# Where the weight slots start in SBUF: byte 64 modulo 128 in every stage instead of in the narrow stages alone

## The reference, cut to what matters

```python
def layer(x, ctx, c, c_ctx, ...):                    # first block, twice
    sh1, sc1, gt1, sh2, sc2, gt2 = adaln(c, w_ada, b_ada)   # silu(c) @ w_ada, 1024 x 6144
    px = modulate(rms_norm(x, g1), sh1, sc1) @ w_in         # 1024 x 1536, for ctx too
    ...                                              # attention, Fourier mix, spatial gate
    x = x + gt1 * (mix @ w_out)                      # 1024 x 1024
    h = modulate(rms_norm(x, g2), sh2, sc2)
    x = x + gt2 * (square(relu(h @ w1)) @ w2)        # 1024 x 4096, 4096 x 1024

def second_block(x, ...):                            # twice
    proj = rms_norm_2(x, attn_norm_g) @ w_in         # 1024 x 3656
    ...                                              # three kinds of causal attention
    x = x + mix @ w_out                              # 1024 x 1024
    h2 = rms_norm_2(x, ffn_norm_g)
    x = x + (silu(h2 @ w_gate) * (h2 @ w_up)) @ w_down   # 1024 x 2816 (two), 2816 x 1024
```

## Time and profile before

| | |
|---|---|
| median of three executions | 1592.0 us |
| the profiled execution | 1594.35 us, span 1592.6 us, mean granted TensorE clock 0.991 |
| TensorE matmuls busy | 1541.2 us, 97% of the span |
| TensorE weight loads busy | 1262.6 us (beside the matmuls) |
| VectorE, ScalarE, GpSimd busy | 1028.4, 795.5, 114.2 us |
| DMA | 322.41 MB, mean 202 GB/s |

### The profile page before, as it was taken

The page is one execution under the profiler, slowest core; times in us unless marked ns, Lnnn a source line. Parts: engine busy times, 40 slices in busy tenths (PEclk is TensorE's granted clock), DMA queues, the critical chain, the costliest instruction groups (busy, mean ns, idle before and its releaser), DMA issues.

```text
span 1592.6 us, 23486 instructions
## 1 busy us (share of the span) xinstructions
PE 1541.2 (97%) x9164; PEld 1262.6 (79%) x9164; DVE 1028.4 (65%) x1577; ACT 795.5 (50%) x1356; POOL 114.2 (7%) x130
## 2 busy tenths in 40 slices
PE   6999999999999999998999999999999999999999
PEld 2864689778888887567898878779998787689987
DVE  3637756455456437576785576978995558879973
ACT  3537735343345225565664456645554456555542
POOL 0111000010001000100000031010000111000000
PEclk9999999999999999999999999999999999999999
DMA  9528623487568524586998689436665596356653
GB/s 360 152 84 313 215 75 114 145 264 253 162 220 277 162 66 133 176 279 190 335 319 300 211 272 312 160 108 183 191 197 191 184 326 227 106 141 192 198 190 115
DMA packets 201005, 322.41 MB, mean 202 GB/s; under 512 B 14576, under 2 KB 100864, under 8 KB 200768
## 3 DMA queue, kind: packets, MB, share of 16 engines
q1 hardware_dynamic: 192992, 293.51, 57.6%
q0 software_dynamic: 7680, 27.34, 4.8%
q10 hardware_dynamic: 224, 0.07, 0.0%
HBM read 298.27 MB, written 22.61 MB: 201 GB/s over the span
## 4 chain that ended last, share of the span: by engine, by line
PE 86%; DVE 7%; DMA 3%; ACT 2%; issue 1%; POOL 0%; SPq 0%; POOLq 0%; DVEq 0%; ACTq 0%
PE bank L2220 53%; PE pair_bank L2220 21%; PE bank L2289 2%; DVE w_lo L1581 1%; PE bank L2537 1%; PE pair_bank L2506 1%; DMA raw<-in_w_in 1%; PE bank L2517 1%; DMA raw<-in_w_ada 1%; PE bank L2315 1%; PE pair_bank L2557 1%; DMA raw<-in_w_mlp 1%; PE bank L2425 0%; PE bank L2571 0%; ACT w_hi L1175 0%
## 5 line engine op out<-in xcount | busy, mean ns | idle before, releaser
L1581 DVE TENSOR_TENSOR w_lo<-raw,w_hi 128x1024 fp32r<-128x1024 f32 (+2 forms) x374 | 447.4, 1218 | 273.5 <-ACT w_hi L1175 272.0
L1175 ACT CAST w_hi<-raw 128x1024 fp32r<-128x1024 f32 (+1 forms) x416 | 428.4, 1045 | 363.2 <-PE bank L2220 236.6
L2220 PE MATMUL pair_bank<-act_hi,w_hi 128*128 128x256 f32 (+1 forms) x744 | 226.8, 305 | 5.0 <-DVE act_lo L1745 2.1
L2220 PE MATMUL pair_bank<-act_hi,w_lo 128*128 128x256 f32 (+1 forms) x744 | 224.7, 302 | 0.0
L2220 PE MATMUL pair_bank<-act_lo,w_hi 128*128 128x256 f32 (+1 forms) x744 | 224.6, 302 | 0.0
L2220 PE MATMUL bank<-w_hi,hid_hi 128*128 128x512 f32 x560 | 220.2, 393 | 0.0
L2220 PE MATMUL bank<-w_lo,hid_hi 128*128 128x512 f32 x560 | 219.6, 392 | 0.0
L2220 PE MATMUL bank<-w_hi,hid_lo 128*128 128x512 f32 x560 | 219.4, 392 | 0.0
L2220 PE MATMUL bank<-w_hi,act_hi 128*128 128x512 f32 (+2 forms) x528 | 206.6, 391 | 8.4 <-DVE w_lo L1581 4.0
L2220 PE MATMUL bank<-w_hi,act_lo 128*128 128x512 f32 (+2 forms) x528 | 200.3, 379 | 0.0
L2220 PE MATMUL bank<-w_lo,act_hi 128*128 128x512 f32 (+2 forms) x528 | 200.1, 379 | 0.0
(11 more groups left out here) (249 smaller groups left out, 2088.9 us busy)
## 6 DMA issues: line engine op xcount, KB each, us to landing
raw<-in_w_mlp SPq DMA_DIRECT2D x128, 512.0 KB, 4.9
raw<-in_w_in SPq DMA_DIRECT2D x112, 512.0 KB, 4.5
raw<-in_w_ada SPq DMA_DIRECT2D x96, 512.0 KB, 5.6
raw<-in_w_gate SPq DMA_DIRECT2D x44, 512.0 KB, 3.8
raw<-in_w_up SPq DMA_DIRECT2D x44, 512.0 KB, 3.8
raw<-in_w_down SPq DMA_DIRECT2D x44, 512.0 KB, 3.6
split_lo<-w_lo POOLq DMA_DIRECT2D x36, 512.0 KB, 5.0
w_lo<-split_lo SPq DMA_DIRECT2D x36, 512.0 KB, 5.1
```

What stands on the lines that cost most here:

```text
L1175: nc.scalar.copy(hi_of(i)[:, 0:w], raw_of(i)[:, 0:w]).then_inc(hi_ready, 1)
L1581: nc.vector.tensor_tensor(lo_of(i)[:, 0:w], raw_of(i)[:, 0:w], hi_of(i)[:, 0:w].bitcast(F32), ALU.subtract).then_inc(lo_ready, 1)
L2220: ins = nc.tensor.matmul(o, a[x], b[y], start=first and i == 0, stop=True, skip_group_check=True)
```

## The change

The rings get slots of exactly 1024 float32, 4096 bytes, and a pad of 64 bytes ahead of them, so that every slot of `raw`, `w_lo`, `w_hi` and `w_hi2` starts at byte 64 modulo 128 (192 modulo 256 for all of them). A second pad of 64 bytes behind them puts all that follows back to byte 0; `w_hi2` gets its place without a pad ahead. The kinds of piece and the function `begins` go. The activations and features stay at byte 0 modulo 128. The order of the instructions on every engine, their shapes and their waits are the same before and after; addresses alone differ.

Of the 512-column fp32r matmuls, 672 (`up1`, layer 0) then have the stationary operand at byte 64 and the moving one at 0, and 3168 have the moving one at byte 64 and the stationary one at 0. The 256-column ones of the narrow stages (2880) stay as they are.

```diff
+        pad("pad_weights", 64, top)
         with ExitStack() as s:
-            raw = sb("raw", [P, RAW, 1024 + 32], F32, s)
-        w_lo = sb("w_lo", [P, RAW, 1024 + 32], F32R)
-        w_hi = sb("w_hi", [P, SPLIT, 1024 + 32], F32R)
+            raw = sb("raw", [P, RAW, 1024], F32, s)
+        w_lo = sb("w_lo", [P, RAW, 1024], F32R)
+        w_hi = sb("w_hi", [P, SPLIT, 1024], F32R)
+        pad("pad_const", 64, top)
...
-            pad("pad_gains2", 64, s)
-            w_hi2 = sb("w_hi2", [P, SPLIT2 - SPLIT, 1024 + 32], F32R, s)
+            w_hi2 = sb("w_hi2", [P, SPLIT2 - SPLIT, 1024], F32R, s)
             sub_g = sb("sub_g", [P, DEPTH], F32, s)
-            pad("pad_sub_g", 96, s)
+            pad("pad_sub_g", 32, s)
...
-        def begins(i):
-
-            return 16 if i < len(n.slots) and n.slots[i][0] == "narrow" else 0
-
-        def raw_of(i):
-
-            return raw[:, i % RAW, begins(i):begins(i) + 1024]
...
-            at_ = begins(i)
             if i < n.first2:
-                return w_hi[:, weights_before(i) % SPLIT, at_:at_ + 1024]
-            if r < SPLIT:
-                return w_hi[:, (weights_before(n.first2) + r) % SPLIT, at_:at_ + 1024]
-            return w_hi2[:, r - SPLIT, at_:at_ + 1024]
+                return w_hi[:, weights_before(i) % SPLIT, :]
+            return w_hi[:, (weights_before(n.first2) + r) % SPLIT, :] if r < SPLIT else w_hi2[:, r - SPLIT, :]
...
-                for dst, src in src_of(raw_of(self.i)):
+                for dst, src in src_of(raw[:, r, :]):
...
-                        self.put("narrow" if l else "w", 1024, lambda r: [(tiles(r, 4), src[:, 4 * q:4 * q + 4, c:c + 256])])
+                        self.put("w", 1024, lambda r: [(tiles(r, 4), src[:, 4 * q:4 * q + 4, c:c + 256])])
```

More of the change, by code:

```diff
@@ L642, in split_at @@
             return (i + lead,)
-        def begins(i):
-            return 16 if i < len(n.slots) and n.slots[i][0] == "narrow" else 0
-        def raw_of(i):
-            return raw[:, i % RAW, begins(i):begins(i) + 1024]
-        def lo_of(i):
-            return w_lo[:, i % RAW, begins(i):begins(i) + 1024]
         def hi_of(i):
             r = (i - n.first2) % SPLIT2
-            at_ = begins(i)
             if i < n.first2:
-                return w_hi[:, weights_before(i) % SPLIT, at_:at_ + 1024]
-            if r < SPLIT:
-                return w_hi[:, (weights_before(n.first2) + r) % SPLIT, at_:at_ + 1024]
-            return w_hi2[:, r - SPLIT, at_:at_ + 1024]
+                return w_hi[:, weights_before(i) % SPLIT, :]
+            return w_hi[:, (weights_before(n.first2) + r) % SPLIT, :] if r < SPLIT else w_hi2[:, r - SPLIT, :]
         def hi_before(i):
@@ L872, in put @@
                     freed(e, self.i - RAW)
-                n.slots.append((kind, used))
-                for dst, src in src_of(raw_of(self.i)):
+                for dst, src in src_of(raw[:, r, :]):
                     e.dma_start(dst, src).then_inc(raw_loaded[r], 16)
                     n.put(f"raw_loaded{r}", self.i)
+                n.slots.append((kind, used))
                 self.known_low(self.i - BEHIND)
@@ L887, in known_low @@
                 self.e.wait_ge(hi_ready, n.at("hi_ready", i))
-                self.e.dma_start(lo_of(i)[:, 0:u].bitcast(F32), split_lo[x, :, 0:u]).then_inc(lo_loaded[r], 16)
+                self.e.dma_start(w_lo[:, r, 0:u].bitcast(F32), split_lo[x, :, 0:u]).then_inc(lo_loaded[r], 16)
                 n.put(f"lo_loaded{r}", i)
@@ L959, in up2 @@
                         for q in range(2):
-                            self.put("narrow", 1024, lambda r: [(tiles(r, 4), src[:, 4 * q:4 * q + 4, j * 256:(j + 1) * 256])])
+                            self.put("w", 1024, lambda r: [(tiles(r, 4), src[:, 4 * q:4 * q + 4, j * 256:(j + 1) * 256])])
             def finish(self):
@@ L1029, in early @@
                 self.e.wait_ge(lo_ready, n.at("lo_ready", i))
-                self.e.dma_start(split_lo[x, :, 0:u], lo_of(i)[:, 0:u].bitcast(F32)).then_inc(lo_stored[i % RAW], 16)
+                self.e.dma_start(split_lo[x, :, 0:u], w_lo[:, i % RAW, 0:u].bitcast(F32)).then_inc(lo_stored[i % RAW], 16)
                 n.put(f"lo_stored{i % RAW}", i)
@@ L1174, in split @@
                         self.e.wait_ge(multiplied, n.at("multiplied", before))
-                nc.scalar.copy(hi_of(i)[:, 0:w], raw_of(i)[:, 0:w]).then_inc(hi_ready, 1)
+                nc.scalar.copy(hi_of(i)[:, 0:w], raw[:, i % RAW, 0:w]).then_inc(hi_ready, 1)
                 n.put("hi_ready", i)
@@ L1580, in split @@
                 self.e.wait_ge(hi_ready, n.at("hi_ready", i))
-                nc.vector.tensor_tensor(lo_of(i)[:, 0:w], raw_of(i)[:, 0:w], hi_of(i)[:, 0:w].bitcast(F32),
+                nc.vector.tensor_tensor(w_lo[:, i % RAW, 0:w], raw[:, i % RAW, 0:w], hi_of(i)[:, 0:w].bitcast(F32),
                                         ALU.subtract).then_inc(lo_ready, 1)
@@ L2237, in parts @@
                 u = n.slots[i][1]
-                return [tiles(v[:, 0:u], k) for v in (hi_of(i), lo_of(i))]
+                return [tiles(v[:, 0:u], k) for v in (hi_of(i), w_lo[:, i % RAW, :])]
             def early(self, x):
@@ L2288, in ada @@
                         j = 32 * (k % 4)
-                        ins = nc.tensor.matmul(bank[bk][j:j + 32, :], cond[:, k, :], tiles(raw[:, r, 0:1024], 2)[:, kk, :],
+                        ins = nc.tensor.matmul(bank[bk][j:j + 32, :], cond[:, k, :], tiles(raw[:, r, :], 2)[:, kk, :],
                                                start=k < 4, stop=True, skip_group_check=True, tile_position=(0, j))
```

## The result

Over 19 executions each, the changed kernel takes 1599.73 us in the median (1593.65 to 1609.15) and the kernel before 1594.22 us (1591.66 to 1599.56). The ratio is 1.0036, 95% interval 1.0023 to 1.0049. The forecast was 1578 us. The profiled execution of the changed kernel took 1600.23 us, span 1598.4 us, against 1594.35 and 1592.6 us. The executions of the changed kernel also spread wider than those of the kernel before, over 15.5 against 7.9 us.

A forecast was written before the change was run, and what follows sets the result against it. TensorE's matmuls, 97% busy, were taken to bound the kernel; gains of 3.2 + 1.1 + 9.9 = 14.2 us took the 1592.0 us median to 1578 us. The forecast's own range was 1573 to 1584, over all cases 1573 to 1610.

The forecast's parts named there:

- the 226.7 ns level: 512-column matmuls: twice the narrow 113.3 ns, seen in some slots (2.72 / 12), expected of all at unequal residues.
- Term 1: up1 of layer 0, 672 matmuls of 512 columns, 231.5 to 226.7 ns: -3.2 us, bounds 0 and 4.0 gained.
- Term 3: Moving weights, 2840 512-column matmuls on the chain, 230.2 to 226.7 ns: -9.9 us, bounds -16.8 and +20.7.
- meeting has no direction: Two SBUF readers meet at equal residues, so exchanging moving and stationary roles should not matter; argued from 119.2 against 113.3 ns.
- Term 2: First pairs of up1 in layer 0, 192 matmuls of 256 columns, each 5.9 ns faster: -1.1 us.
- the rival of 1608 us: Down, out and rows stages: moving weights at byte 64 go to 237.5 ns, 16.4 us lost net; chance 0.27.
- The mild case of the last rival: Down, out and rows stages: moving weights at byte 64 go to 234.2 ns, 11.4 lost less 4.3 gained; chance 0.06.
- Term 4: Narrow stages, 2880 matmuls of 256 columns: same residues modulo 128 as before, so 0.
- Terms 5 and 7: VectorE and ScalarE splits at byte 64: 0; DMA into slots at byte 64: 0, bound 1.4 us.
- The estimate of 3 us: DMA part of the chain: rows of 2048 bytes go from a mean of 66 to 70 beats, 6%.
- Term 6: adaLN matmuls reading raw at byte 64, 2.4% of the chain: 0, with 1.7 us allowed either way.
- The sign I had: mv_ik, 328 moving columns: pieces at byte 64 and byte 0 both take 0.45 us per three matmuls; counted as doubt.

The follow-up runs named there:

- e1: Kernel before with every piece at byte 64 modulo 128, in slots of 4224 bytes that alternate between 64 and 192 modulo 256; 1597.94 us, ratio 1.0030.
- e2: Kernel before with only up1 of layer 0 starting its pieces at byte 64, in slots of 4224 bytes; 1593.41 us, ratio 0.9998.
- e7: e4 with narrow pieces always 64 bytes behind instead of 64 and 192 in turn; 1585.5 us, ratio 0.9942 to the kernel before.
- e3: Changed kernel's 4096-byte slots moved to byte 0 modulo 128; rings, act, hid1 at 128 modulo 256, hid2 at 0; 1601.74 us, ratio 1.0047.
- e4: Kernel before with 4352-byte slots, wide pieces and activations at 128 modulo 256, narrow pieces 64 and 192 bytes behind in turn; 1579.8 us, ratio 0.9911.
- e8: e4 with the first 256-column pairs of up1 in layer 0 also at the narrow offset; 1583.2 us, ratio 0.9928 to the kernel before.

## Why the prediction was wrong, point by point

**The step that failed** is the choice of the 226.7 ns level for 512-column matmuls at unequal residues (terms 1 and 3, 13.1 of the 14.2 us). The reasoning was that 256 columns gain at a distance of 64, that "meeting has no direction", and that the undisturbed pace of wide ones must therefore be reached the same way. Measured at distances of 64 and 192, wide matmuls take 228.9 or 233.3 ns, in either role (down stages after, up1 after, e1, e2). They do reach 226.7, but at a distance of 0 modulo 256, which the change took away from the half of the slots that had it. For 256 columns it is the other way round: 0 is worst with 120.0, and 64 or 192 good with 113.3.

**Term 1**, up1 of layer 0, -3.2 us: it became 672 x 1.8 = 1.2 us of loss (231.5 to 233.3 ns). Its bounds held nothing below zero, because I took the arrangement for known. It was known at another width only.

**Term 2**, the first pairs, -1.1 us: right, 5.44 us for 48 as foretold.

**Term 3**, moving weights, -9.9 us: the down stages gained 0.6 ns in some places (88.15 to 87.91 us for 384) and lost 2.4 to 3.0 in others (81.74 to 82.59 for 354; 60.81 to 61.60 for 264). Over all back-to-back matmuls of this kind the distance of the starts is 230.3 ns in the mean in both profiles, so the term came to about nothing. That is within the bounds I gave, near their middle, not at the end I chose. The upper bound, and the rival of 1608 us with it, rested on a misread row: the twelve at 978.59 us are not a pace of 237.5 ns. Their starts stand 229 and 237 or 238 ns apart in turn (978.72 to 981.05 for ten, 233 in the mean); a longer gap at each end makes up the rest. The mild case of the last rival, 1599 us with a chance of 0.06, has the right time and a wrong mechanism: its 234.2 ns on all moving weights never came, and up1 lost where it should have gained.

**Term 4**, the narrow stages, 0: the largest single loss, 4.6 us in the profiled execution. "Same residues modulo 128 as before" was true and not enough. The slots had stopped alternating modulo 256, and with that went what takes the stream out of its slow pace: shown by e1 and e7, and by the slots in which the pace was kept or left; that it is left, and not merely less often entered, is what nine stages out of nine and none out of three say. Why a change of residue does it is open.

**Terms 5 and 7**, splits and DMA, 0: right, 1220 and 1047 ns, 309 GB/s at a share of 0.94. The estimate of 3 us that the prediction made from the Trainium skill, DMA: Bandwidth & Descriptors, section "How a descriptor splits into AXI transactions", has no counterpart here: in the wide stage from 337 to 425 us, where slots at 0 and 128 became slots at 192, the share stayed at 0.72.

**Term 6**, adaLN, 0: its share of the chain stayed at 2.4%.

**The sign I had**: the 328-column rows of mv_ik said that byte 64 brought a moving operand nothing. I counted it as doubt and still gave the forecast 0.45. And the earlier trace rows held the evidence against the modulus: runs of twelve at 2.72 and 2.81 us in one kind of stage differ in their residues modulo 256. By the kernel's own layout the twelve at 265.32 us have both parts of the weights at distance 0, those at 286.83 the high part at 128 and the low part at 0.

The rule of the Trainium skill, SBUF — State Buffer, section "Who interferes with whom", by which moving operand and weight load read independently, would make all these kernels alike but for noise. e3 and e4 differ by 22 us, and by addresses alone; against this reading of the rule, that no address matters, the measurement decides. Why a distance costs what it does, whether the meeting is in SBUF or in TensorE's own readers, no run here shows.

## What to carry to other kernels

When a trace shows that an address matters for one shape, find the modulus and the width by grouping the same instruction by its addresses before carrying the number to another shape; here the trace of before already held two of the four distances at 512 columns. Streams of back-to-back fp32r matmuls on this chip liked equal residues modulo 256 at 512 columns (226.7 ns), and a distance of 64 or 192 that changes from slot to slot at 256 columns (113.3 ns). A ring whose slots all have one residue can hold a slow pace for a whole stage. Runs that scatter more after a change of layout can be a hint of it, but not more: e1, whose slots alternate, scatters by 8.9 us over 8 runs, and the 4.7 us of a slow stage explain only a part of the changed kernel's 15.5.

## What the runs showed of the hardware that I had not expected

The spacing of fp32r matmuls with a weight load each, at a granted clock of 1.00, by the distance between moving and stationary operand modulo 256:

| columns | distance 0 | 128 | 64 or 192 |
|---|---|---|---|
| 512 | 226.7 to 226.8 ns (e3, e4) | 232.4 (e3) | 228.9 or 233.3 with fixed slots (after); 230.9 and 232.5 alternating (e1) |
| 256, activations at 128 throughout | 120.0 (e3) | not measured by itself | 113.3, or 117.8: for a whole stage with fixed slots (after, e7), for four slots at most with alternating ones (e4, e8) |

That two executions of one program put the 117.8 ns stage in different layers, 4.7 us each time, is the second thing: a deterministic program with a time that has memory of how its stream began.
